# An encoder layer on one core: in the output stage VectorE splits the last two gate units and the first two tiles' sums and norms are interleaved

## The reference

```python
x = x + hier_moe(rmsnorm(x, g_ffn), ...)        # two weighted expert rows per token
x = x + sigmoid(rmsnorm(x, g_ple) @ w_ple_gate) * (p @ w_ple_proj)
return rmsnorm(x, g_final)
```

## Time and profile before

| what | value |
|---|---|
| median of 3 runs | 1792.2 us (1790.76, 1792.2, 1797.99) |
| profiled execution, its own time | 1789.94 us |
| profiled execution, span from first to last instruction | 1788.1 us |
| TensorE busy | 1679.0 us, 94% of the span |
| VectorE busy | 906.0 us, 51% |
| ScalarE busy | 592.5 us, 33% |
| GpSimd busy | 410.8 us, 23% |
| mean granted TensorE clock | 0.974 of full speed |

### The profile page before, as it was taken

The page is one execution under the profiler, slowest core; times in us unless marked ns, Lnnn a source line. Parts: engine busy times, 40 slices in busy tenths (PEclk is TensorE's granted clock), DMA queues, the critical chain, the costliest instruction groups (busy, mean ns, idle before and its releaser), DMA issues. The chain is left out here.

```text
span 1788.1 us, 26258 instructions
## 1 busy us (share of the span) xinstructions
PE 1679.0 (94%) x10034; PEld 1384.6 (77%) x10035; DVE 906.0 (51%) x991; ACT 592.5 (33%) x1017; POOL 410.8 (23%) x285
## 2 busy tenths in 40 slices
PE   7999999999999989999989999997899999996997
PEld 7878888877877767777878887885777777784786
DVE  5202777202134137742899226224768889941674
ACT  5211222231111136642344335113544443443332
POOL 1011111111211101003200121000356565652330
PEclk9999999999999999999789999998999999998999
DMA  6211222323456312017865434234767778733452
GB/s 224 78 54 60 80 79 80 107 84 115 133 182 191 103 66 66 28 52 241 255 198 140 165 124 139 82 95 172 253 219 271 274 285 305 283 129 141 142 188 94
DMA packets 117130, 267.17 MB, mean 149 GB/s; under 512 B 13027, under 2 KB 60851, under 8 KB 117036
## 3 DMA queue, kind: packets, MB, share of 16 engines
q1 hardware_dynamic: 101068, 211.08, 36.0%
q0 software_dynamic: 8320, 30.43, 5.2%
q10 hardware_dynamic: 7648, 24.35, 3.8%
HBM read 194.27 MB, written 71.55 MB: 149 GB/s over the span
## 5 line engine op out<-in xcount | busy, mean ns | idle before, releaser
L2224 DVE TENSOR_TENSOR ex_wlo<-ex_raw,ex_whi 128x1024 fp32r<-128x1024 f32 x102 | 162.2, 1591 | 10.6 <-ACT ex_whi L2218 7.3
L2802 PE MATMUL rt_p<-ex_whi,ex_xh 128*128 x280 | 113.6, 406 | 15.6 <-DVE ex_wlo L2224 8.9
L2220 DVE CAST ex_whi<-ex_raw 128x1024 fp32r<-128x1024 f32 x96 | 107.8, 1123 | 40.3 <-DMA ex_raw<-experts 36.6
L271 PE MATMUL rest_p<-hi_h,whi_in 128*128 128x512 f32 (+1 forms) x480 | 121.2, 361 | 0.0
L271 PE MATMUL rest_p<-lo_h,whi_in 128*128 128x512 f32 (+1 forms) x480 | 119.6, 357 | 0.0
L271 PE MATMUL rest_p<-hi_h,wlo_in 128*128 128x512 f32 (+1 forms) x480 | 119.6, 357 | 0.0
L2804 PE MATMUL rt_p<-ex_whi,ex_xl 128*128 x280 | 109.9, 392 | 0.0
L2803 PE MATMUL rt_p<-ex_wlo,ex_xh 128*128 x280 | 109.7, 392 | 0.0
L271 PEld LDWEIGHTS rest_p<-hi_h,whi_in 128*128 128x128 f32 x480 | 79.7, 188 | 21.6 <-issue 7.6
L945 POOL TENSOR_TENSOR wlo_in<-wraw_in,whi_in 128x1024 fp32r<-128x1024 f32 x18 | 43.9, 2439 | 227.4 <-ACT whi_in L908 227.3
L914 ACT ACTIVATE rest_out<-rest_p 128x1024 f32<-128x1024 f32 x20 | 20.5, 1026 | 214.2 <-PE rest_p L271 210.6
(11 more groups left out here) (415 smaller groups left out, 3992.2 us busy)
## 6 DMA issues: line engine op xcount, KB each, us to landing
ex_raw<-experts SPq DMA_DIRECT2D x96, 512.0 KB, 6.2
wraw_in<-units SPq DMA_DIRECT2D x36, 512.0 KB, 4.2
y_slots<-ex_y ACTq DMA_DIRECT2D x35, 512.0 KB, 4.1
rest<-rest_out SPq DMA_DIRECT2D x20, 640.0 KB, 5.6
scan_e<-erow SPq DMA_DIRECT2D x32, 256.0 KB, 4.8
xtok<-conv_tok SPq DMA_DIRECT2D x10, 640.0 KB, 3.4
z_x<-x SPq DMA_DIRECT2D x10, 512.0 KB, 4.0
ao_gate<-rest SPq DMA_DIRECT2D x8, 640.0 KB, 5.9
```

What stands on the lines that cost most here:

```text
L271: mm = pe.matmul(out[:, n, 0:size], w[:, kk, :], h[:, kk, c:c + size], start=(kk == 0 and w is whi and h is hi), stop=(kk == ktiles - 1 an ...
L2220: eng.tensor_copy(self.hi[:, e % 2, n, :], self.raw[e % 2][:, n, :]).then_inc(self.w_hi[n], 1)
L2224: eng.tensor_tensor(self.lo[:, e % 2, n, :], self.raw[e % 2][:, n, :], self.hi[:, e % 2, n, :].bitcast(F32), ALU.subtract).then_inc(self.w ...
L2802: pe.matmul(gu[s][:, :], xh[s][:, kk, :], hi, start=(kk == 0), stop=False)
```

## The change

VectorE now makes both parts of the gate units 6 and 7, as soon as each has been loaded. ScalarE's two copies are gone. In VectorE's queue the second tile's sum is cut in two: its first half goes ahead of the first tile's `scale`, its second half behind the first tile's `apply`. The waits and semaphores are otherwise those of before, and the other engines' queues are as they were.

```diff
-    def split_hi(self, act, n):
-        act.wait_ge(self.w_in[n - 6], 16)
-        act.activation(self.hi[n][:, :], self.raw[n][:, :], ACT.Copy).then_inc(self.w_hi, 1)
-
-    def split_lo(self, eng, n):
-        eng.wait_ge(self.w_hi, n - 5)
-        eng.tensor_tensor(self.lo[n][:, :], self.raw[n][:, :], self.hi[n][:, :].bitcast(F32), ALU.subtract).then_inc(self.w_lo, 1)
+    def split(self, dve, n):
+        dve.wait_ge(self.w_in[n - 6], 16)
+        dve.tensor_copy(self.hi[n][:, :], self.raw[n][:, :]).then_inc(self.w_hi, 1)
+        dve.wait_ge(self.w_hi, n - 5)
+        dve.tensor_tensor(self.lo[n][:, :], self.raw[n][:, :], self.hi[n][:, :].bitcast(F32), ALU.subtract).then_inc(self.w_lo, 1)
...
-            for n in (6, 7):
-                w.split_hi(act, n)
             square(0)
             square(1)
             split(0)
...
-            def combine(t):
-                for n, view in enumerate((first, second)):
+            def combine(t, ways=(0, 1)):
+                for n in ways:
+                    view = (first, second)[n]
...
-            w.split_lo(dve, 6)
-            w.split_lo(dve, 7)
+            w.split(dve, 6)
+            w.split(dve, 7)
             combine(0)
+            combine(1, (0,))
             norm.scale(dve, 0)
-            combine(1)
             norm.apply(dve, 0, x[:, 0, :], xn[0][:, :])
+            combine(1, (1,))
             norm.scale(dve, 1)
             norm.apply(dve, 1, x[:, 1, :], xn[1][:, :])
```

## The result

| | executions | median us | range us | ratio to before |
|---|---|---|---|---|
| before | 22 | 1794.15 | 1790.76 to 1799.78 | |
| after | 22 | 1798.45 | 1790.18 to 1806.6 | 1.0024, interval 1.0013 to 1.0036 |

In this comparison the changed kernel is slower, by 4.3 us: inside the 0.5% that the prediction held for the limit of a measurement, but above its range (1789 to 1797). The profiled execution took 1800.64 us, its span is 1798.8 us, its mean granted clock 0.969 (0.974 before).

The account below looks back on a forecast made before the run. TensorE, busy 94% of the span, was taken as the bound, with the second tile's norm setting the output stage's start. Splits 0, order -0.15, clock 0 gave -0.15 us: 1789.8 profiled, 1792.1 as median; range 1789 to 1797.

Parts of the forecast that it names:

- Taking the copies from ScalarE: Ahead of the first sum: removing two ScalarE copies, 2.00 us in sum, is worth nothing on the path.
- the rival that the root keeps its 1.54 us: GpSimd's `root(0)` stays at 1.54 us, not 0.56; `apply(1)` 0.83 us later, time 1793.0; chance 0.05.
- The earlier first norm: `apply(0)` 1.84 us earlier; rival counts it in full, 1790.4; chance 0.08, with or without the gather's 0.6.
- the sign of being wrong: Tile 0's product starting over 1.5 us earlier or later against the first sum would show the prediction wrong.
- The 0.76 us of issue ahead of the first gather: GpSimd's first gather: if VectorE's low parts delay it, up to 0.6 us returns; taken as 0.
- cost 0: GpSimd's last low part: unit 6's CAST lets it end at 1630.7, as before; bounds 0 and 1.1 us.
- the same dip: TensorE's clock from 1658 to 1662, behind the idle time between turns: same loss as before, 1.7 us; change 0.
- twice as long: TensorE's clock dip behind the turns doubles: +1.7 us, time 1793.8; chance of the clock either way 0.12.
- 0.15 us earlier: VectorE's `apply(1)` at 1656.3 instead of 1656.47; `turn(1)` and the product move by the same 0.15 us.
- So it starts at once, 1649.7: VectorE's first half of sum 1 starts when its gather lands, at 1649.7, and ends at 1651.0.
- The cover of 1.22 us: VectorE's idle time while ScalarE squared, just wide enough for sum 1's first half; `scale(0)` stays at 1650.99.
- the port: Rival at GpSimd's last low part: unit 6's subtraction runs then, +1.1 us, time 1793.2; chance 0.2.

Follow-up runs that it names:

- before again: The kernel before, unchanged, measured again: 1793.99 us, ratio 0.9994.
- split only: Against the changed kernel, the queue order of before is restored, so only VectorE's splits of gate units 6 and 7 remain: 1794.38 us, again 1796.09; ratio 1.0009 both times.
- turn inside 2: Against the changed kernel: splits delayed, `turn(1)` inside tile 0's product, `rest(0)` ahead of `apply(1)`, tile 2's sum, norm and square moved earlier: 1793.13 us, ratio 0.9996.
- split late: Against the changed kernel, VectorE's splits wait until the experts' last `down` product has read its operand: 1795.64 us, ratio 1.0013.
- after again: The changed kernel, unchanged, measured a second time: 1792.79 us, ratio 1.0006.
- after filled: Against the changed kernel, three more warm-up products between `turn(0)` and `turn(1)`: 1793.38 us, ratio 1.0005.
- before filled: Against the kernel before, two more warm-up products between `turn(0)` and `turn(1)`: 1791.62 us, ratio 0.9995.
- after, third: The changed kernel, unchanged, measured a third time: 1796.40 us, ratio 1.0022.
- Order only: Against the kernel before, only the new order of VectorE's sums and norms, without the moved splits: 1793.16 us, ratio 1.0006; again 1794.43 us, 0.9999.
- before padded: Against the kernel before, two tiny VectorE memsets of unused numbers at the output stage's head: 1789.87 us, ratio 0.9983.

## Why the prediction was wrong

Over the first comparison and the four later ones after's mean is 1796.14 us (70 executions). Over the first set of before, the four later ones and before again, before's is 1793.52 (173 executions; one of 2789 us is left out). That is +2.62 us with a standard error of 0.60, so 1.4 to 3.8; without the first comparison on either side it is +1.74 (standard error 0.65). Where the clock is on record (70 executions against 151) 1.7 us (0.7) of the difference is lost clock and 1.0 us (0.4) is the rest. By the traces some 1.8 us should come from three terms of the prediction's sum, which are named below; the rest stays open.

**Right.** Taking the copies from ScalarE gave nothing that shows: split only's S to end (138.55, 137.24) lies within before's (139.63, 137.22). `root(0)` is 0.56 to 0.57 us once VectorE has nothing to run beside it, so VectorE's operation had held it, and the rival that the root keeps its 1.54 us falls. The earlier first norm is worth nothing while `turn(1)` stands ahead of the product: `apply(0)` came 0.7 to 1.7 us earlier against S in the new order, and the product 10.55 to 11.99 us behind S, where the old order has 10.46 to 10.70; so it stayed within the 1.5 us that the prediction named as the sign of being wrong. Where the order was changed so that it counts (turn inside 2), the product did come 1.0 us earlier. The 0.76 us of issue ahead of the first gather are still there with the low parts long done. The chain of waits of the changed kernel:

```profile
1647.43 4.31 DMA y_slots<-ex_y
...
1651.78 0.76 issue
1652.54 0.98 POOL g_first L2986
```

So they don't come from VectorE, and leaving them out of the sum was right.

**Wrong: "cost 0" for the splits.** "I take 0, since the measured landing puts the CAST there, by a margin of only 0.1 us." The mechanism and both its prices held, but the margin was smaller than what the landing varies by. Of the eight traces of kernels that split early, the subtraction began ahead of `ex_al` in four (by 0.01, 0.06, 0.23 and 0.28 us), and `ex_al` took 1.80, 1.75, 1.58 and 1.52 us. In the other four it began 0.03 to 0.15 us behind, and `ex_al` took 0.72 or 0.73. The ten traces without an early split, three of them with split late's wait, all have 0.72. It reaches the path, for TensorE's last `down` product waits for it, in before:

```profile
1630.86 0.69 PE L2817 MATMUL pp_p<-ex_whi,ex_ah 128*128 x1 [2.35 <-POOL ex_al L2766]
```

and in after again:

```profile
1632.18 0.79 PE L2817 MATMUL pp_p<-ex_whi,ex_ah 128*128 x1 [3.43 <-POOL ex_al L2766]
```

This wait is 2.35 or 2.36 us in the fourteen traces and 3.15 to 3.43 in the four. The first gather starts 12.08 to 13.62 us behind `ex_al`'s start in the four, and 10.08 to 11.98 in the other fourteen; the two lowest of these, 10.08 and 10.09, are those in which the clock did not fall in that product. The mean of the four is 1.66, 0.94 longer than 0.72; if half of the executions lie on each side, as half of the traces do, the term should have been +0.5 (an estimate). The rule of the Trainium skill (SBUF — State Buffer, Who interferes with whom) is an exclusive lock. For VectorE in a two-port mode the page gives it for the whole instruction to whoever issues first; of an instruction with two inputs in SBUF, as this subtraction is, it says that it contends with GpSimd's reads. A lock of that kind fits both outcomes here: whoever begins first makes the other wait, `ex_al` until 0.59 us behind the subtraction, or the subtraction until it takes 1.65 us.

**Wrong: "the same dip" of the clock, 0 us.** In the old order TensorE idles 1.75 us between the `turn`s, and six traces lost 3.2, 1.5, 3.1, 1.5, 1.7 and 3.7 us of full speed behind S: the dip comes in half of them, and the trace of before that I predicted from had it. In the new order it idles 2.40 to 3.45 us, and the dip came in all eight (3.1 to 4.1); in three of them, after idle times of 3.44 and 3.45 us (lost 4.0, 3.8 and 4.1), it was the prediction's dip "twice as long". The prediction saw the longer idle time, and named the dip a rival, but carried over one trace as if it were fixed. The mean difference is 1.1 us (3.6 less 2.5). That the idle time causes it is supported by the fill, in one trace of each kernel: after filled is the only one of nine traces in the new order without the dip (0.9 us lost). Before filled has none either (1.5), which half of the old order's traces have anyway.

**Wrong: "0.15 us earlier" for `apply(1)`.** "So it starts at once, 1649.7": the first half of sum 1 was to start 1.2 us behind S. It started 1.25 to 2.34 us behind it in nine traces, in eight of them after VectorE had waited 0.10 to 1.05 us for the gather to land. The cover of 1.22 us was just wide enough for one landing, and too narrow for the others. `apply(1)` stands 8.00 to 9.03 us behind S there, mean 8.30, against 7.98 to 8.00 in the seven of the old order: +0.3 us and not -0.15. The late landings are not the whole of it. In the one trace without such a wait (after, third) `apply(1)` stands at 8.00, where the steps of the prediction give 7.81: `apply(0)` is at 3.41 and not 3.31, as the hand-over from `root(0)` to it, which the prediction put at nothing, took 0.11 us, and shorter ones behind it make up the other 0.09.

The last two together should be some 1.4 us. S to end measured a mean of 138.2 us in six traces of the old order without fill and 139.5 in eight of the new, +1.3 (standard error 0.5). With the port's 0.5 that is 1.8 us, within the interval of the +2.62. The times of the two halves alone confirm this sum only in part (24 executions of each against 69 of before on the same chips). Order only should be some 1.4 us slower, and is 0.9 (standard error 1.0), with 0.3 us (0.9) less lost clock. Split only should be 0.5 us slower by the port, and is 2.3 (0.8), of which 2.2 (0.9) is lost clock.

**Wrong: the range.** 1789 to 1797 took before's three runs for its time. In 22 its median is 1794.15, 2 us higher; the rest of the 6.35 us by which 1792.1 was off is this comparison's difference of 4.3, of which the three terms above account for some 1.8. After's medians in the four later sets are 1792.79 to 1796.40, all within the range; the first, over more executions, was not.

**Open.** What remains of the 2.62, about 0.8 us, and of the first comparison's 4.3, shows at none of the changed places. In 18 traces the last `ex_al` starts at 1630.0 to 1642.4, with 32.4 to 44.4 us of clock lost up to it (correlation 0.65; 0.66 between time and lost clock over before's 151 executions). One and the same kernel takes part in this: before lost 32.4 and 41.0, after 44.4, 37.5, 42.7, 39.3 and 42.7. One such place, in windows of before:

```profile
394.00:404.00 10.00, 8.15 (x39) 6.25 (x40) 0.68 (x1) 3.92 (x9) 3.62 (x3) 1.00 0.41 78
```

and of before again:

```profile
394.00:404.00 10.00, 7.74 (x33) 5.55 (x28) 0.68 (x1) 4.28 (x9) 2.92 (x3) 0.83 0.35 62
```

In both, TensorE had just waited 2.26 us for ScalarE. After has 0.66 in these 10 us, and after again 1.00. The executions suggest that the moved splits make such dips likelier. Over all comparisons but the first, the kernels in which VectorE makes the high parts lost 1.7 us more than the others (120 executions against 211, standard error 0.5), and more on each of the four chips; up to the last `ex_al` their eleven traces lost 40.5 us in the mean and the seven others 36.8 (standard error of the difference 1.7). This grouping was made after the fact, and no run shows how an edit in the last stage would cause it. Both controls, which shift VectorE's queue or take the copies from ScalarE but keep the high parts off VectorE, lost 2 us less than before; that speaks against the mere place of the code as the cause.

No version beats before: before filled stands at 0.9995 and before padded at 0.9983, with intervals that hold 1.

## What to carry to other kernels

An order in one queue that brings the first tile forward and the second back pays only if the engine behind starts on the first; here `turn(1)` ahead of the product made the second tile the price, and gave TensorE a longer idle time as well. Where an operation is moved next to another engine's on a shared lock, and the margin between them is smaller than the spread of a DMA's landing, count both outcomes. And a clock dip, or its absence, read in one trace is a sample: take it from several traces before it stands as a term.

## What was not expected of the hardware

Executions of one and the same kernel differ by 16 us and more (after, 1790.18 to 1806.6; turn inside 2, 1785.15 to 1803.89), in part by dips of TensorE's clock behind the same wait of 2.26 us in some of them and not in others. Behind 1.75 us of idle time between the two `turn`s the clock fell in three of six executions, behind 2.40 us and more in all eight, and behind 2.35 us ahead of the last `down` product in twelve of fourteen. One contended pair costs whichever engine begins second: a subtraction of 1.23 us took 1.65 to 1.78 when GpSimd began 0.03 to 0.15 us ahead of it.
